# A transformer block with retrieved experts: paired gathers multiplied in turn, and the chain and the attention units of a tile moved to other groups

## What is computed

```python
def block(tb):                     # tb: 128 tokens (a tile), rmsnorm'd
    q = (tb @ w_query).reshape(128, 8, 2, 64)
    s = jnp.einsum('thpd,hpnd->thpn', q, sub_keys)
    s1, i1 = lax.top_k(s[:, :, 0], 16)
    s2, i2 = lax.top_k(s[:, :, 1], 16)
    cand_s = s1[..., :, None] + s2[..., None, :]
    cand_i = i1[..., :, None] * 128 + i2[..., None, :]
    top_s, pos = lax.top_k(cand_s, 16)
    idx = jnp.take_along_axis(cand_i, pos, axis=-1)
    g = jax.nn.softmax(top_s, axis=-1)
    act = gelu(jnp.einsum('thk,td->thk', expert_u[idx], tb))
    return jnp.einsum('thk,thkd->td', g * act, expert_v[idx])
# ahead of it: h = h + concat(rmsnorm(o_a), rmsnorm(o_b)) @ w_out, where
# o_a is stick-breaking attention (causal), o_b sliding-window attention with sinks
```

## Time and profile before

| | us |
|---|---|
| median of 3 runs | 3155.91 |
| lowest and highest | 3152.45, 3156.11 |
| the profiled execution | 3157.37 |
| its span, first to last instruction | 3155.6 |

### The profile page before, as it was taken

One profiled execution on the slowest core, in us unless ns is written; L12 is line 12 of the kernel. 1 busy time (PEld: TensorE's weight loads), 2 busy tenths in 40 slices (PEclk: granted clock), 3 DMA queues, 4 the chain that ended last, 5 costly groups with the idle time before them and its releaser, 6 DMA issues.

```text
span 3155.6 us, 30250 instructions
## 1 busy us (share of the span) xinstructions
PE 2397.4 (76%) x8606; PEld 1118.7 (35%) x8606; DVE 2081.8 (66%) x4959; ACT 1459.3 (46%) x3733; POOL 1348.4 (43%) x1134
## 2 busy tenths in 40 slices
PE   8999847898778857896789868896775577555655
PEld 5677723432343223432243223332342234222222
DVE  2120686677768867686758876786758775876544
ACT  3051144497337733584439833694432333232222
POOL 0000034454455544454445544554345435455453
PEclk9999969999799979998889988998898888878787
DMA  3541289999999999999999999999999999999997
GB/s 117 182 128 51 72 349 382 418 351 373 410 409 411 383 405 416 407 393 387 410 418 366 375 415 418 387 373 394 391 420 421 421 401 414 421 420 419 420 421 325
DMA packets 200227, 1143.41 MB, mean 362 GB/s; under 512 B 23584, under 2 KB 59760, under 8 KB 68736
## 3 DMA queue, kind: packets, MB, share of 16 engines
q0 software_dynamic: 147456, 1073.81, 84.0%
q1 hardware_dynamic: 52608, 67.71, 6.4%
HBM read 1126.34 MB, written 15.07 MB: 362 GB/s over the span
## 4 chain that ended last, share of the span: by engine, by line
PE 35%; DMA 31%; DVE 15%; ACT 9%; issue 6%; POOL 4%; POOLq 0%; SPq 0%; ACTq 0%; DVEq 0%
DMA r_uv<-in_experts,r_wk 30%; PE ps L1515 14%; DVE r_uv L1200 7%; PE ps L1293 5%; POOL r_uv L620 4%; PE ps L1452 4%; PE ps L1254 3%; PE ps L1317 2%; ACT r_wk L851 2%; PE ps L1323 2%; ACT r_uv L854 1%; ACT L643 1%; PE ps L1329 1%; ACT L843 1%; PE ps L1336 1%
## 5 line engine op out<-in xcount | busy, mean ns | idle before, releaser
L1515 PE MATMUL ps<-r_uv 128*64 128x512 f32 x4096 | 1443.2, 721 | 682.8 <-ACT r_uv L854 669.5
L620 POOL DMA_INDIRECT r_uv<-in_experts,r_wk x1024 | 1239.6, 1211 | 1542.3 <-PE ps L1515 1210.9
L1200 DVE CUSTOM_DVE_ANT_0 r_uv<-r_uv,hnrep 128x1024 f32<-128x1024 f32 x1024 | 1256.0, 1244 | 641.5 <-DMA r_uv<-in_experts,r_wk 634.2
L1515 PEld LDWEIGHTS ps<-r_uv 128*64 128x64 f32 x4096 | 502.1, 156 | 1419.7 <-ACT r_uv L854 958.2
L843 ACT ACTIVATE r_wk<-r_wk 128x2 f32<-128x2 f32 x512 | 104.2, 203 | 1353.0 <-DVE r_wk L1200 1351.5
L854 ACT ACTIVATE r_uv<-cst,r_wk 128x64 f32<-128x64 f32 x1024 | 300.5, 340 | 16.7
L851 ACT ACTIVATE r_wk<-r_wk 128x1 f32<-128x1 f32 x1024 | 245.9, 287 | 16.8
L843 ACT ACT_TABLE_LOAD x158 | 202.7, 1283 | 2.9
L643 ACT ACT_TABLE_LOAD x147 | 188.6, 1283 | 6.4 <-PE ps L1445 1.4
L1469 PEld LDWEIGHTS ps<-r_wk,r_wq 128*128 128x128 f32 x1024 | 120.6, 193 | 48.4 <-issue 48.2
L1469 PE MATMUL ps<-r_wk,r_wq 128*128 128x128 f32 x1024 | 131.3, 282 | 0.0
(11 more groups left out here) (154 smaller groups left out, 2010.7 us busy)
## 6 DMA issues: line engine op xcount, KB each, us to landing
r_uv<-in_experts,r_wk POOLq DMA_INDIRECT x1024, 11.3
r_wk<-lkv_dram SPq DMA_DIRECT2D x72, 128.0 KB, 7.1
hnrep<-in_w_chunks SPq DMA_DIRECT2D x16, 512.0 KB, 3.7
r_uv<-in_x SPq DMA_DIRECT2D x8, 512.0 KB, 3.3
h2cur<-in_w_chunks SPq DMA_DIRECT2D x8, 512.0 KB, 3.7
r_wo<-in_w_out SPq DMA_DIRECT2D x8, 512.0 KB, 5.1
r_wk<-in_x SPq DMA_DIRECT2D x8, 512.0 KB, 7.9
r_wq<-in_w_query SPq DMA_DIRECT2D x8, 512.0 KB, 4.2
```

The costliest lines, as they stand in the source:

```text
L620: g.indirect_dma_start(uv[:, k % NB, :], None, experts, bass.IndirectOffsetOnAxis(idx[b % 2][:, k:k + 1], 0)).then_inc(rows_in[k % NB], 16)
L1200: v.tensor_tensor_reduce(uv[:, k % NB, 0:D], uv[:, k % NB, 0:D], hnrep[:, k % GRP, :], 1.0, 0.0, ALU.mult, ALU.add, actv[:, k:k + 1]).then ...
L1515: last = t_.matmul(ps[HALF * (k % GRP):HALF * (k % GRP) + HALF, i, :], uv[:, k % NB, 0:HALF], uv[:, k % NB, D + 512 * i:D + 512 * i + 512] ...
```

## The change

1. **PE, within a group.** Before, gather k's two matmul calls came, then gather k + 1's, each behind its own wait, and a late unit's first scores stood between the two. Now one wait covers both diagonals, the calls alternate between the two gathers, and the unit's first scores stand ahead of the pair. Both slots are freed after the second half.
2. **Tile 0** is routed like the others: heads 0 to 3 are picked and gated in the front, heads 4 to 7 in its own groups (`at_own`). The list of pieces is in another order and has a hole of six steps (`GAP`), in which the chain of tile 0 stands alone.
3. **The chain of the next tile** stands in PE's groups 3 to 26 instead of 4 to 33, with up to two mix or query steps in a group. DVE's tops start at group 29 instead of 36.
4. **Late units** start at group 28 and are spread over 29 groups (`28 + 29 * u // n`), instead of from 34 over 24.

```diff
-LATE_AT = {f: [34 + 24 * u // len(units) for u in range(len(units))] for f, (g, units) in LATE.items()}
+LATE_AT = {f: [28 + 29 * u // len(units) for u in range(len(units))] for f, (g, units) in LATE.items()}
...
-          + [(m, p, 1, 4) for p in range(PAIRS) for m in (QA, KA)] + [(QB, p, 1, 4) for p in range(PAIRS)])
+          + [(QA, 0, 1, 4), (KA, 0, 1, 4), (QA, 1, 1, 4), (KA, 1, 1, 4), (QA, 2, 1, 4)]
+          + [(QB, p, 1, 4) for p in range(PAIRS)] + [(KA, 2, 1, 4), (QA, 3, 1, 4), (KA, 3, 1, 4)])
...
-HEAD_AT = (0, 2, 4, 5, 7, 9, 10)
+GAP = (26, 32)
+PIECE_AT = {i + (GAP[1] - GAP[0] if i >= GAP[0] else 0): i for i in range(NP)}
+NS = max(PIECE_AT) + 1
...
-                    if b == 0:
-
-                        if k % TOPK == 0:
-                            gate(pool, "pool", head_ready, k // TOPK + 1)
-                    elif k == 0:
-                        gate(pool, "pool", idx_ready, b)
-                    elif k == K // 2:
-                        gate(pool, "pool", idx_ready2, b)
+                    if k == 0:
+                        gate(pool, "pool", idx_ready, b + 1)
+                    if k == K // 2:
+                        gate(pool, "pool", idx_ready2, b + 1)
...
-            at = {7: "exp", 10: "pT", 13: "ob", 14: "oa", 15: "r2", 20: "h2sq", 23: "hnT", 32: "qT", 34: "keys",
-                  58: "gexp"}
+            at = {5: "exp", 8: "pT", 10: "ob", 11: "oa", 13: "r2", 17: "h2sq", 20: "hnT", 25: "qT", 27: "keys",
+                  56: "gexp"}
...
-            at = {6: "mask", 8: "norm", 11: "pT", 16: "r2", 19: "h2", 21: "hn", 40: ("scores", 0), 42: ("numbers", 0),
-                  57: ("gate", 0), 60: ("routed", 0)}
+            at = {4: "mask", 6: "norm", 8: "pT", 14: "r2", 16: "h2", 18: "hn", 37: ("scores", 0), 39: ("numbers", 0),
+                  55: ("gate", 0), 58: ("routed", 0)}
             for h in range(4):
-                at.update({36 + h: ("top", h), 44 + 4 * h: ("pick", h), 46 + 4 * h: ("top", 4 + h)})
-
-            at_own = {1: ("scores", 1), 5: ("numbers", 1), 12: ("pick", 4), 14: ("pick", 5), 17: ("pick", 6),
-                      20: ("pick", 7), 23: ("gate", 1), 26: ("routed", 1)}
+                at.update({29 + 2 * h: ("top", h), 42 + 4 * h: ("pick", h), 44 + 4 * h: ("top", 4 + h)})
+
+            at_own = {1: ("scores", 1), 2: ("numbers", 1), 10: ("pick", 4), 12: ("pick", 5), 20: ("pick", 6),
+                      22: ("pick", 7), 23: ("gate", 1), 26: ("routed", 1)}
...
+            at0 = {7: "mask", 9: "norm", 10: "pT", 23: "r2", 24: "h2", 25: "hn", 36: ("scores", 0), 37: ("numbers", 0),
+                   42: ("gate", 0), 44: ("routed", 0)}
+            for h in range(4):
+                at0.update({32 + h: ("top", h), 38 + h: ("pick", h), 45 + h: ("top", 4 + h)})
...
-            at = {4: "scores", 9: "pT", 12: "pv", 13: "ssq", 22: "hnT", 33: "keys"}
-            at.update({14 + i: ("mix", i) for i in range(4)})
-            at.update({24 + i: ("query", i) for i in range(PH)})
+            at = {3: ["scores"], 7: ["pT"], 9: ["pv"], 12: ["ssq", ("mix", 0)], 13: [("mix", 1), ("mix", 2)],
+                  14: [("mix", 3)], 19: ["hnT"], 26: ["keys"]}
+            at.update({21 + i: [("query", 2 * i), ("query", 2 * i + 1)] for i in range(4)})
...
+                    if late is not None:
+                        for u in late_units(late, n):
+                            late_scores(b, late, u, 0)
+                    if n == 0:
+
+                        pe.wait_ge(h3_ready, b + 1)
+                    pe.wait_ge(diag_ready, K * b + GRP * n + GRP)
+                    for i in range(2):
+                        for j in range(GRP):
+                            slot = (GRP * n + j) % NB
+                            last = t_.matmul(ps[HALF * j:HALF * j + HALF, i, :], uv[:, slot, 0:HALF],
+                                             uv[:, slot, D + 512 * i:D + 512 * i + 512], start=n == 0, stop=n == NG - 1)
+                            if i == 1:
+                                last.then_inc(rows_used, 1)
+                    if more:
+                        for step in at.get(n, ()):
+                            tile_step(step, b + 1)
```

118 lines of the change are left out of this document (35 added, 83 removed).

## The result

| | before | after |
|---|---|---|
| median of the runs, us | 3156.01 (3152.45 to 3159.48, 4 runs) | 3136.70 (3133.58 to 3140.94, 4 runs) |
| ratio after / before | | 0.9941, 95% interval 0.9929 to 0.9952 |
| profiled execution, us | 3157.37, span 3155.6 | 3133.58, span 3131.8 |
| mean granted clock of TensorE | 0.889 | 0.854 |

The change makes the kernel 19 us faster, 0.6%. The forecast was 44 us, 3112. The time lies inside its range (3078 to 3150), but outside the span of the forecast's own case (3095 to 3130); of the cases that the prediction laid out the second rival comes closest, in which VectorE and ScalarE take over from TensorE (3145).

The account below looks back on a forecast made before the run. Gathers at 421 GB/s were the floor, with PE and ACT over it in tile 3's late stretch. 3157.4 less 53 (late units) and 17 (tile 0), plus 24.5 (chain) and 1.5 (start), gave 3113.4 profiled, 3112 median; range 3078 to 3150.

Parts of the forecast that it names:

- the forecast's own case: Whole kernel: all terms roughly as reckoned, with the denser chain costing 0.9 to 6 us per tile; 3095 to 3130, 52%.
- second rival: Late stretches: DVE and ACT take over from PE, giving back only 26 us; denser chain costs 30; 3145 in all, 15%.
- The floor: Every tile: gathers can't go faster than tile 7's 421 GB/s, 2.515 us each, whatever the engines do.
- Part 1: PE in late groups: alternation gains nothing; scores ahead of the pair save PE 34 us in tile 3, showing little alone.
- Part 2: Late stretches of tiles 0 to 4: with units over 29 groups, losses fall from 76 to 23 us, gain 53.
- Part 3: Tile 0's groups 0 to 36: routed like the others, gain 17 us; first gather 1.5 us later, between 0 and 4.
- Part 4: Next tile's denser chain, tiles 0 to 6: PE falls behind the DMA's cover, losing 3.5 us per tile, 24.5 together.
- Rival 3: Mix and query groups: the compressed chain starves the DMA at 10 us per tile; slower, 3168, chance 10%.
- The sum: Whole kernel: 3157.4 - 53 - 17 + 24.5 + 1.5 = 3113.4 us in the profiled execution, 3112 as a median.
- Rival 1: Denser chain: the DMA's cover holds, so it costs nothing, and late stretches gain 5 us more; 3081, chance 18%.
- Rival 4: PE's gather pairs: alternation shortens every pair, so the denser chain costs nothing; 3087, chance 5%.
- a low clock: PE in late stretches: stays below the floor even at tile 5's clock, 0.81 of full instead of 0.99.

Follow-up runs that it names:

- e14: Changed kernel with a pair's gathers multiplied gather by gather, scores still ahead and one wait for both diagonals: 3143.59 us, ratio 0.9955.
- e2: Kernel before with only the new pair order (gathers in turn, unit's scores ahead, one wait): 3155.89 us, ratio 1.0003.
- e3: Changed kernel with the old pair order (gather by gather, scores between): 3129.43 us, ratio 0.9917.
- e1: Changed kernel with TensorE's running sums three groups after a unit's scores, not two, and GpSimd's add one group later: 3119.59 us, ratio 0.9896.
- e8: e6 with work left out: four VectorE picks per tile, except the first, without their three wide passes: 3103.63 us, ratio 0.9836.
- e10: e6 with VectorE's step for the next tile (pick, search) ahead of the softplus: 3116.13 us, ratio 0.9861.
- e6: Changed kernel with sums at three groups; in tiles 0, 3 and 4 weights at five and units in two of three groups: 3125.42 us, ratio 0.9897.
- e17: e13 with units at even distances over 29 groups and weights at four groups, as in the changed kernel: 3149.09 us, ratio 0.9965.
- e12: Kernel before with work left out: four VectorE picks per tile, except the first, without their three wide passes: 3146.37 us, ratio 0.9971.
- e15: Kernel before with only tile 0 routed like the others and the order of pieces this needs: 3144.39 us, ratio 0.9962.
- e16: e15 with the sums three groups after the scores and VectorE's step ahead of the softplus: ratio 0.9973.
- e13: e18 with VectorE's four second-half searches moved to groups 1, 2, 3 and 5 of the tile itself: 3113.10 us, ratio 0.9864.
- e9: e6 with VectorE's picks in tiles 0, 3 and 4 moved to groups without a softplus, and the searches moved too: 3151.86 us, ratio 0.9984.
- e18: e10 with the old pair order (gather by gather, scores between): 3108.68 us, ratio 0.9853.

## Why the prediction was right or wrong

**The floor** (2.515 us a gather, 421 GB/s) held: tile 7 takes 318.4 us at 420 GB/s.

**Part 1: right in its mechanism.** The alternation gains nothing (e14: same clock, and a time that can't be told from that with turns), and TensorE saves about what was reckoned, 29 us in e2 where 34 were put down. The prediction gave part 1 no gain of its own ("A faster PE alone therefore shows little, for ACT is next"), and e2 measured none; the expectation that put 8 to 15 us a tile on it as the forecast's step went beyond the prediction. The reason was another one, though: what came next was not ScalarE's load but 26.5 us of waiting for the softplus. The prediction named that wait in its second rival ("PE's sums wait for a softplus that waits for ACT's logs") and gave it 15%. It also had the new order needed for part 2; without it the changed kernel is no slower (e3, 0.9917).

**Part 2: the step that failed, 53 us forecast and 21 measured** (26 by the lengths). It failed where busy time was compared with the floor engine by engine: "PE then stands below the floor", "ACT falls below the floor", 139 of 156.5 for VectorE, and the rest called waits that mostly go with the load, so that only 23 us were left of 76. It was 56. ScalarE's load came out as reckoned (150.2 us in tile 3's stretch, which has two groups more than the 147.1 were for) and VectorE's no higher (139.4), but three engines at 83 to 90% of the floor that hand a unit back and forth in fixed groups didn't reach it. 4 us were left to such waits in tiles 3 and 4 each; it was 8.3 and 9.6. In tiles 1 and 2, where ScalarE had slack, 1 us each was left, and it was 12.9 and 9.4: there the cause is shown, since the sums one group later brought these losses down to 4.4 and 3.6 (e1). In tile 0, 13 were left and it was 16.2. For tiles 0, 3 and 4 the cause is shown only in part. With the later sums and ScalarE's groups shared, VectorE's load in groups 42 to 56 and its wait for the logs hold them (e8, e10, made on e6); in the changed kernel as it is, covering that wait gave nothing while the weights stood one group behind the sums (e17). So more than one hand-over is tight there, and which ends last in the changed kernel stays open. The row that should have warned is the earlier trace rows: in tile 3 DVE is busy 123 of a floor of 125 even before it waits for anything.

**Part 3: right.** Tile 0's groups 0 to 28 lost 163.3 x 53 / 421 = 20.6 us before and 148.3 x 15 / 421 = 5.3 after, a gain of 15.3 of the forecast 17; alone the part measured 12 (7 to 17) with the start inside it. The first gather is at 391.3, 3.0 us later; 1.5 was taken, between 0 and 4.

**Part 4: right in size, and not isolated by a run.** In groups 0 to 28 of tiles 1 to 6 the loss rose from 24.1 to 36.2 us by the same formula, 2.0 a tile where 3.5 was forecast. The profiles of all the runs put it somewhat higher: the five kernels with the old chain (the kernel before, e2, e12, e15, e16) need 887 to 897 us for these stretches, 891 on average, and the fifteen with the denser one 898 to 914, 908 on average, which is 2.8 a tile (in e13 and e17 of them these stretches hold VectorE's searches too). Rival 3 is out.

**The sum.** By their lengths the stretches account for the whole difference of the two profiled executions: -25.7 in the late stretches of tiles 0 to 4, -15.0 in tile 0's groups 0 to 28, +11.2 in those of tiles 1 to 6, +2.0 up to tile 0's group 0, and +3.7 in all the rest (the last four groups of tiles 0 to 5 are 0.2 of it, tile 5's late stretch 1.5), together -23.8. The medians differ by 19.3; the changed kernel's profile is of its fastest execution.

**Rival 2** had the late stretches give back 26 and 3145 in all. It is nearest to what happened in them (21 by the formula, 26 by the lengths), and its price for part 4 (30) was too high. The late stretches gave 32 us less than forecast; that the time still lies in the range is in part because part 4 cost less, 12 to 17 us in tiles 1 to 6 where 21 were forecast. Rival 1 is out, since part 4 does cost. Rival 4 is out by e14, which has no alternation and a time that can't be told from the change's. Rival 1's 3081 leaves out the later start; with it, it would be 3082.5.

The Trainium skill (TensorE: Matmul & The Clock Gate, "What's actually happening") says that TensorE's throttled state is the default and that activity releases it. The runs agree: with 29 us less of TensorE's busy time in tile 3's late stretch, the granted clock of the stretch goes from 0.95 to 0.89 (e2). The prediction had named a low clock and put it at no cost.

## What to carry to other kernels

Busy time against a floor says which engine can't be the reason, not that the floor will be reached: where several in-order engines hand one unit around in fixed steps, look at the whole chain of hand-overs (here scores, logs, softplus, sums, weights), give each step slack, and watch that slack for one hand-over isn't taken from the next (e17). Where a step waits, work that is ready can stand ahead of it (e10, 11 us by the ratios). Look at the load group by group as well as over the stretch (e9 moved nothing out of the stretch and cost 27 us). And before shortening the engine that looks fullest, ask which engine's output it will then stand and wait for. The fastest kernel here, e18 with 3108.68 us, 28 us below the changed kernel, combines four edits: sums one group later, logs and weights in shared groups with the weights one group later, VectorE's step ahead of the softplus, and part 1 undone. The first gave 14 us alone. The second gave nothing by itself, and without it the first and third were 32 us slower (e17 against e13).

## What was unexpected of the hardware

TensorE's clock answers to a change that only packs its work. Every kernel with the scores ahead of the pair and one wait for both diagonals shows a mean granted clock of 0.84 to 0.86, every other 0.88 to 0.90. In tile 3's late stretch the first of the sums (L1323) took 614 ns a matmul in the kernel before and 669 with part 1 alone, the second (L1329) 590 and 690. So these got 9 and 17% longer, 5 us together, out of the 32 us that the packing saved on the pairs. The queries in the same stretch stayed at 281 ns.

Two gathers multiplied into the two column halves of the array run side by side whether they are written in turns or one after the other: eight matmuls in 1.95 us in e14, 1.94 in turns in the changed kernel. They fall apart when a unit's scores stand between them.
